# Differential attention as one pipeline over heads, placed between the query and value weights of a two-block transformer kernel

## What is computed

```python
h = rms_norm(x, g_pre_mix[1])
k, v = shared_kv(x, g_kv, w_kv)                       # rms_norm(x, g_kv) @ w_kv, split into k and v
q = (h @ w_q)                                         # 8 heads, 2 halves of 64, per head
logits = einsum(q, k) * scale + bias[dist]            # for each half m = 0, 1
logits = where(dist >= 0, logits, -inf)
probs = softmax(logits)
attn = probs[:, :, 0] - lam * probs[:, :, 1]
o = rms_norm(attn @ v, subln_g) * (1.0 - lambda_init) # per head
mix = o @ w_o
x = x + rms_norm(mix, g_post_mix[1])
```

## Time and profile before

| what | us |
|---|---|
| median of 3 runs | 1398.59 |
| lowest and highest | 1395.29 to 1399.53 |
| profiled execution | 1391.52 |
| its span | 1389.5 |
| PE busy, share of the span | 96% |
| DVE busy | 66% |
| ACT busy | 52% |

### The profile page before, as it was taken

How to read it: one execution, slowest core, us unless ns; L and a number is a source line. 1 busy time by engine, 2 the same in 40 slices (tenths; PEclk the granted TensorE clock), 3 DMA queues, 4 the chain that set the end, 5 groups by cost and what they waited for, 6 DMA issues and landing times.

```text
span 1389.5 us, 25078 instructions
## 1 busy us (share of the span) xinstructions
PE 1330.0 (96%) x10558; PEld 1288.7 (93%) x10558; DVE 918.8 (66%) x1505; ACT 725.1 (52%) x1219; POOL 4.5 (0%) x13
## 2 busy tenths in 40 slices
PE   5998899999998999999999999999999999999996
PEld 5897679999998999999999999999987799999996
DVE  4687655765446777444875999746564546999654
ACT  5754234665332666334545666646453446666644
POOL 1000000000000000000000000000000000000000
PEclk9999979999999999999999999999898999999997
DMA  6232005555552465654753666663272133666630
GB/s 257 85 122 81 31 3 150 182 180 170 181 170 75 145 200 175 194 183 129 227 180 118 194 187 196 200 200 106 89 246 66 31 109 106 201 193 192 204 121 31
DMA packets 58415, 205.20 MB, mean 148 GB/s; under 512 B 6328, under 2 KB 8640, under 8 KB 58048
## 3 DMA queue, kind: packets, MB, share of 16 engines
q1 hardware_dynamic: 56816, 201.77, 46.0%
q10 hardware_dynamic: 1488, 1.85, 0.5%
HBM read 202.53 MB, written 1.06 MB: 147 GB/s over the span
## 4 chain that ended last, share of the span: by engine, by line
PE 85%; DVE 8%; ACT 5%; issue 1%; DMA 1%; ACTq 0%; DVEq 0%
PE PS L340 65%; PE PS L385 7%; PE PS L351 2%; PE PS L368 2%; PE PS L419 2%; PE PS L2020 1%; PE PS L2019 1%; ACT WH L318 1%; DVE WL L325 1%; PE PS L466 1%; PE PS L652 1%; DMA HB<-bias_rows 1%; DVE Z L1417 1%; PE PS L784 0%; PE PS L690 0%
## 5 line engine op out<-in xcount | busy, mean ns | idle before, releaser
L325 DVE TENSOR_TENSOR WL<-RAW,WH 128x1024 fp32r<-128x1024 f32 (+2 forms) x383 | 460.5, 1207 | 261.5 <-ACT WH L318 261.2
L318 ACT ACTIVATE WH<-RAW 128x1024 fp32r<-128x1024 f32 (+2 forms) x383 | 391.2, 1042 | 251.3 <-PE PS L340 222.0
L340 PE MATMUL PS<-UH,WH 128*128 128x256 f32 (+1 forms) x1624 | 462.9, 285 | 6.9 <-DVE UL L1402 3.0
L340 PE MATMUL PS<-UH,WL 128*128 128x256 f32 (+1 forms) x1624 | 462.6, 285 | 0.0
L340 PE MATMUL PS<-UL,WH 128*128 128x256 f32 (+1 forms) x1624 | 462.4, 285 | 0.0
L340 PEld LDWEIGHTS PS<-UH,WH 128*128 128x128 f32 x1624 | 309.1, 190 | 7.9 <-issue 4.7
L340 PEld LDWEIGHTS PS<-UH,WL 128*128 128x128 f32 x1624 | 309.1, 190 | 0.0
L340 PEld LDWEIGHTS PS<-UL,WH 128*128 128x128 f32 x1624 | 307.5, 189 | 0.0
L340 PE MATMUL PS<-HL,WH 128*128 128x272 f32 (+1 forms) x512 | 145.8, 285 | 0.0
L340 PE MATMUL PS<-HH,WH 128*128 128x272 f32 (+1 forms) x512 | 145.7, 284 | 0.0
L340 PE MATMUL PS<-HH,WL 128*128 128x272 f32 (+1 forms) x512 | 145.4, 284 | 0.0
(11 more groups left out here) (346 smaller groups left out, 1976.9 us busy)
## 6 DMA issues: line engine op xcount, KB each, us to landing
RAW<-wpack SPq DMA_DIRECT2D x365, 512.0 KB, 3.6
RAW<-wpack SPq DMA_DIRECT2D x16, 384.0 KB, 3.5
X<-xin SPq DMA_DIRECT2D x1, 1088.0 KB, 5.1
C<-cst SPq DMA_DIRECT2D x1, 1072.0 KB, 10.0
HB<-bias_rows ACTq DMA_DIRECT2D x1, 1024.0 KB, 7.4
out<-X SPq DMA_DIRECT2D x4, 256.0 KB, 2.3
RAW<-wpack SPq DMA_DIRECT2D x2, 256.0 KB, 3.5
PI<-pin ACTq DMA_DIRECT2D x2, 256.0 KB, 3.1
```

Source lines behind the costliest of these rows:

```text
L318: a.e.activation(WH[n % NH][:, 0:w], RAW[n % NR][:, 0:w], ACT.Copy).then_inc(*a.mark("wh", n))
L325: v.e.tensor_tensor(WL[n % NH][:, 0:w], RAW[n % NR][:, 0:w], WH[n % NH][:, 0:w].bitcast(f32), ALU.subtract).then_inc(*v.mark("wl", n))
L340: ins = t.e.matmul(o, part(n, hw, kw, a, b), x(kx), start=first and not i and not p, stop=last and i == len(kcs) - 1 and p == 2)
```

## The change

1. **Order of weights**: for each group of 256 columns, one query unit, two value units, one query unit, in place of all value units and then all query units.
2. **Keys and queries are split.** DVE multiplies the key with the root into `TQ` (a slot of `TMA`, four in turn), ACT copies it to `KHH`, DVE subtracts to `KHL`; for queries `QHH` and `QHL` (three slots). The bias read back is split to `HBH` and `HBL`. `scores` becomes five fp32r matmuls in place of two fp32 ones, for each half and each of two row blocks.
3. **One loop over heads**, `for s in range(9)`: query(s), turn(s-2), scores(s-1), value(s), attend(s-2) on PE. The bias matmul stands before the keys and its DMAs early in the key stage. `AA` is gone: the combination overwrites `EE`.
4. **In the key stage** ACT and DVE each go unit by unit through weight split, key parts and query operand.
5. **Output by heads**: the first four output units run at once, feature block by feature block (`output`), with turn, attend and normed of the last heads between them; the other four follow as before.
6. **Embedding step**: its last pair of blocks goes through sigmoid, product and square one block at a time, its gain (`embed_gain`) moves behind the root; the first 40 fillers are gone, 12 stand between `root_begin` and `root_end`.

The diff, cut to its core:

```diff
@@ weight_units
             proj("k", "w_kv_2", None, 0, 1024)
-            rows("v", "w_kv_2", None, 1024, 2048)
-            proj("q", "w_q_2", 0, 0, 1024)
+            for g in range(4):
+                proj("q", "w_q_2", 0, 256 * g, 256 * g + 128)
+                rows("v", "w_kv_2", None, 1024 + 256 * g, 1280 + 256 * g)
+                proj("q", "w_q_2", 0, 256 * g + 128, 256 * g + 256)
@@ scalar_ffn
+                square(a, f"ple{layer}", 1, u, MM2[:, 2 * u:2 * u + 2, :], S)
+                embed_gain(a, layer, u)
+            def last_step():
...
+                for m in range(2):
+                    a.wait_ge("gz", layer, 3, m)
+                    a.e.activation(TMA[:, 2 + m, 0:S], TMA[:, 2 + m, 0:S], ACT.Sigmoid).then_inc(*a.mark("sig", layer, 3, m))
...
+                for m in range(2):
+                    a.wait_ge("pg", layer, 3, m)
+                    a.e.activation(SQ[1][:, m, 0:S], MM2[:, 6 + m, :], ACT.Square).then_inc(*a.mark("sq", ple, 3, m))
@@ tensor_diff
-            keep_going(t, 40)
-            root_sum(t, "ple0", 1, S, ("mr", "kv", 6))
+            root_begin(t, "ple0", 1, S, ("mr", "kv", 6))
             banks.hold(("root", "ple0"))
+            keep_going(t, 12)
+            root_end(t, "ple0", 1, S)
             root_spread(t, "ple0", S)
-            keep_going(t, 18, "ple0")
+            t.e.matmul(PS[0:8, b, 0:384], RBX[:, :], HOT, start=True, stop=True).then_inc(*t.mark("dif", "gr"))
+            keep_going(t, 16, "ple0")
...
-            root_spread(t, "kv", S)
             for j in range(8):
                 if j > 3:
+                    b = banks.take(t, ("k", j), ("tq", j))
                     products(t, PS[:, b, 0:S], n0 + j, pairs, 0, 128, uh, ul, u_ready).then_inc(*t.mark("dif", "k", j))
+                if j == 4:
+                    root_spread(t, "kv", S)
...
-                        t.e.matmul(o, c2("anti"), hb, start=True, stop=False)
-                        ins = t.e.matmul(o, QH[ps_, h, q0:q0 + 128], KH[ps_, h, 0:w], start=False, stop=True)
+                    for o, q0, k0, w in ((PS[:, b0 + m, 0:128], 0, 128, 128), (PS[:, b0 + m, 128:384], 128, 0, 256)):
+                        t.e.matmul(o, ANTI[:, :], HBH[:, h, k0:256], start=True, stop=False)
+                        t.e.matmul(o, ANTI[:, :], HBL[:, h, k0:256], start=False, stop=False)
+                        for p, (q_, k_) in enumerate(((QHH, KHH), (QHL, KHH), (QHH, KHL))):
+                            ins = t.e.matmul(o, q_[ps_, h % 3, q0:q0 + 128], k_[ps_, h, 0:w], start=False, stop=p == 2)
...
+            for s in range(9):
+                if s < 8:
+                    query(s)
+                if s > 1:
+                    turn(s - 2)
+                if s:
+                    scores(s - 1)
+                if s < 8:
+                    value(s)
+                if s > 1:
+                    attend(s - 2)
+
+            normed(0)
+            normed(2)
...
+            output(range(0, 4))
+            turn(7)
             normed(4)
+            output(range(4, 6))
+            attend(7)
+            keep_going(t, 16, done=("t", 7))
             normed(6)
+            keep_going(t, 12, done=("t", 7))
+            output(range(6, 8)).then_inc(*t.mark("omm", "do", 1, 0, 1))
...
+            tensor_output(t, "mix", "do", ("mr", "ffn1", 6), uh, ul, o_ready, first=2)
@@ scalar_diff
+            act_split(a, n0 + 6)
             root_sqrt(a, "kv", S)
+            act_split(a, n0 + NH)
             root_keep(a, "kv", 0, S)
             for j in range(8):
...
+                if j:
+                    act_split(a, n0 + j + NH)
+                high("k", j, KHH[:, j, :])
+                split_hi(a, ("qx", j), XH[:, j, :], X_(j), g("gpm1", j))
...
+            for s in range(9):
+                if s < 8:
+                    if s % 2 == 0:
+                        act_split(a, unit_at["q", s] + NH)
...
+                    high("q", 8 + s, QHH[:, s % 3, :])
+                if s in (0, 2):
+                    bias(2 * s)
+                if s > 1:
+                    turn(s - 2)
+                if s == 8:
+                    roots(0, 6)
+                if s:
+                    scores(s - 1)
+                if s < 8 and s % 2 == 0:
+                    act_split(a, unit_at["v", s] + NH)
+                if s < 8:
+                    value(s)
+                if s > 1:
+                    attend(s - 2)
+                if s < 8 and s % 2:
                     act_split(a, unit_at["q", s] + NH)
@@ vector_diff
+            for j in range(8):
+                if j:
+                    dve_split(v, n0 + j + NH)
+                v.wait_ge("dif", "k", j)
+                v.wait_ge("rk", "kv")
...
+                v.e.tensor_tensor(TQ(j), PS[:, banks.at["k", j], 0:S], RR[0][:, 0:S], ALU.mult).then_inc(*v.mark("tq", j))
+                if j:
+                    split_lo(v, ("qx", j - 1), XL[:, j - 1, :], X_(j - 1), g("gpm1", j - 1), XH[:, j - 1, :])
+                low(j, KHL[:, j, :], KHH[:, j, :], "khl", j)
+            split_lo(v, ("qx", 7), XL[:, 7, :], X_(7), g("gpm1", 7), XH[:, 7, :])
...
+            for s in range(9):
+                if s < 8:
+                    if s % 2 == 0:
+                        dve_split(v, unit_at["q", s] + NH)
+                    query(s)
+                if s in (0, 2):
+                    bias(2 * s)
+                if s:
+                    scores(s - 1)
+                if s < 8:
+                    low(8 + s, QHL[:, s % 3, :], QHH[:, s % 3, :], "qhl", s)
+                    if s % 2 == 0:
+                        dve_split(v, unit_at["v", s] + NH)
                 if s == 8:
+                    roots(0, 6)
+                    scaled(0)
+                if s:
+                    combine(s - 1)
+                if s > 1:
+                    attend(s - 2)
+                if s < 8 and s % 2:
+                    dve_split(v, unit_at["q", s] + NH)
```

342 lines of the change are left out of this document (174 added, 168 removed).

## The result

| | before | now |
|---|---|---|
| median, us | 1396.9 (4 runs) | 1410.7 (4 runs) |
| lowest and highest | 1394.3 to 1399.5 | 1407.7 to 1412.7 |
| profiled execution | 1391.5 | 1407.7 |
| its span | 1389.5 | 1405.9 |
| PE, DVE, ACT busy | 96%, 66%, 52% | 95%, 66%, 52% |

The ratio of the times is 1.0097, with a 95% interval of 1.0068 to 1.0125. The two profiled executions differ by 16.2 us, the medians by 13.8. Slower was the likeliest side of the forecast, and 1410.7 lies just inside the upper edge of its range (1411). But its middle, 1401.7, is 9 us short, and those 9 us need an explanation.

The account below looks back on a forecast made before the run. PE was taken to bound the kernel. Terms -22.6 + 16.2 + 1.85 + 2.8 + 3.7 + 1.85 + 0 + 0.3 - 1.0 = +3.1 us on the median before, 1398.6, gave 1401.7; range 1394 to 1411.

Parts of the forecast that it names:

- straight work, a head's scores: PE, heads: 2.24 us for a head's scores in place of 4.0; all straight work up to last scores -22.6 us.
- entry and key stage, start of value 0: First embedding step +0.3 us; key stage +16.2 us, since query(0) waits for the last XL until 1028.0.
- clock behind it: PE's clock falls behind the key stage's wait and again behind the wait at s = 2: +1.85 us each.
- wait at s = 2: Loop over heads: DVE's subtractions, query and second bias half delay the maxima, so turn(1) holds PE for +3.7 us.
- waits at s = 4, 6, 8: Loop over heads: 0.8 us of wait at s = 4 and 6, 1.2 us at s = 8; together +2.8 us.
- clock in the last scores: Last scores of the loop: no clock fall charged there, 0 us.
- tail: Last scores to last output sums: 45.6 us against 45.7, so 0, between -4 and +2.
- end: End of the kernel: gain copies and half a square leave the path to the root, -1.0 us (-0.6 to -1.5).
- ACT and DVE taking turns: Key stage: the two engines work one after the other, 3.49 us a round for seven rounds.
- one between the halves of the output products: Tail: third output group waits for banks 0 and 1 until ACT has read them, 3.4 us.
- Rival A: Scores: narrow fp32r matmuls cost a plain fp32 pass, 0.21 us; +8.0 us, 1409.7 in all; chance 0.25.
- the size of a clock fall: PE's clock: 1.85 us lost wherever PE starves for over 2 us, taken from the two queries behind an earlier gap.

Follow-up runs that it names:

- e3: Changed kernel with each head's 20 score matmuls reordered: bias ones in two groups of four, query by key ones in two groups of six; median 1398.7 us, ratio 1.0018.
- e7: Changed kernel with all eight XH and XL made before the root of the key stage, nothing else moved; median 1405.0 us, ratio 1.0055 to the kernel before.
- e2: Changed kernel with value block 0 in front of query 0 on PE; median 1413.9 us, ratio 1.0128 to the kernel before.
- e4: Changed kernel with the second half of the bias split at s = 3 and DVE's value unit subtraction behind the combination; median 1402.3 us, ratio 1.0041.
- e12: Changed pipeline with plain fp32 scores, early XH and XL, copies ahead, value unit moved, other banks, reordered tail; median 1387.7 us, ratio 0.9947 to the kernel before.

## Why the prediction came out as it did

The sum was +3.1 us, the profiled difference is +16.4. Term by term:

| term | forecast | measured | how seen |
|---|---|---|---|
| straight work, a head's scores | 2.24 us | 3.62 | 8 x 1.38 = +11.0 over the forecast |
| entry and key stage, start of value 0 | 1028.3 | 1029.3 | +1.0; a round is 3.39 us, forecast 3.49 |
| clock behind it | 1.85 | 0.6 | value 0 takes 3.57 us, the others 2.95: -1.2 |
| wait at s = 2 | 3.7 | 1.97 | -1.7 |
| clock behind it | 1.85 | 4.4 | 10.2 us at 1.2 GHz: +2.6 |
| waits at s = 4, 6, 8 | 2.8 | 2.25 | -0.6 |
| clock in the last scores | 0 | 0.8 | 4.44 us in place of 3.63: +0.8 |
| tail | 0 | -0.2 | from the last scores to the sums 45.5 us, before 45.7 |
| end | -1.0 | -1.2 | -0.2 |

The corrections add up to 11.5 us, with the 3.1 to 14.6 of the 16.4. Of the other 1.8 us, 0.8 are the second half of a change of height: the next value matmul starts 0.23 us behind the first (1039.61 to 1039.84) in place of 0.12, at seven blocks that stand behind a head's scores. Another 0.5 are five queries behind a product with V (2.83 us or more in place of 2.73), where the height stays and the width changes, and 0.4 are query 1 (3.15 us).

**Right.** That the gain of the heads' straight work is eaten in the key stage, by ACT and DVE taking turns, with the period to 0.1 us; PE's largest wait in sum for `XL` (8.9 us in four waits, though the longest single one, 2.61 us, is for `MM` in the tail); a wait before the second turn and one between the halves of the output products released by ACT (2.46 us, forecast 3.4); a tail that comes out even.

**The step that failed** is the price of a head's scores. "A head's scores are 10 fp32r matmuls of 256 columns, 0.114 us each, and 10 of 128 columns" put together prices from runs of *like* matmuls. The two prices are right: the transposes of the earlier trace rows gave the narrow one well. The 81 ns that the Trainium skill gives for the form ("TensorE: Matmul & The Clock Gate", section "Back-to-back issue gap") isn't seen here: 0.11 us. What has no term is the mix of 128 and 64 rows: each change costs 0.15 to 0.21 us, and there are 8 in a head. None of the rivals was this. Rival A came nearest in time (its mark was 3.2 us a head) and was wrong in cause: it took the narrow form to be dear. That 1410.7 still lies inside the range is luck in this sense: the range reached that far for rival A's sake. The rows of before held a hint that I passed over: a narrow plain pair with the bias, then one by query and key, 0.31 and 0.42 us, unlike prices for equal columns. The same changes of height stand in the scores of before.

**The second** is the size of a clock fall. I charged 1.85 us each time, from a stretch of queries. Those rows catch only the end of it. The window from where the clock fell, in the trace of the kernel before:

```profile
1041.10:1051.30 10.20, 10.20 (x31) 0.50 0.14 58
```

The clock was down for 10.2 us there too, first over head 0's scores (7.01 us in place of 4.08) and then over half of the two queries. By these rows the fall had cost 2.9 + 1.85, some 4.8 us, much like the 4.4 behind the turn at s = 2. The prediction had taken the slow scores out of the old time and charged only the queries' part for each new fall. Such stretches aren't all alike: behind e3's wait of 3.89 us PE was at 1.2 GHz for 6.8 us, behind e7's of 11.73 for 11.4. What sets their length isn't shown.

**What I had wrong about the key stage**, although its total fitted: that `XL` alone held PE. e2 and e7 show that the way to `QHL` of the first head held it equally.

## What to carry to other kernels

Count changes of height between neighbouring matmuls, not only matmuls: order a block so that operands of equal height stand together, and matmuls on disjoint halves of the rows as neighbours; that alone gave back 11 of 16 us here. Before filling an idle stretch or removing a wait, follow the helpers' chains to the *next* thing the busy engine will want; if that is equally late, the gain turns into a wait, and a wait of 2 us cost twice its own length again in clock (4.4 us behind 1.97). Price a fall of the clock from where it falls to where it is back, not from the part that looks cleanest. In a stage where two engines hand each operand back and forth, let one run a step ahead and serve the first consumer first.

## What the hardware showed that I hadn't expected

- A matmul of 64 rows next to one of 128 rows: 0.15 us for each change when the next has 128 columns, 0.19 to 0.21 when it has 256 (fp32r; 3.62, 3.10 us a head with 8, 4 changes). At each change the weight load starts with its matmul, not 0.06 us or more ahead.
- Two matmuls on rows 0 to 63 and 64 to 127, into different banks, start within 0.01 us of each other and overlap; twelve take 0.89 us.
- PE busy without a gap, on a turn, scores and what follows, stayed at 1.2 GHz for 10.2 us, behind a wait of 1.97 us; so it did in the kernel before behind one of 2.25. Over the same work without the wait in front (e4) the clock stayed up.
- The same instructions ahead of this stage ended up to 5.0 us apart in the traces of different kernels (first key matmul 985.25 in the changed kernel, 990.27 in e12), so a gain of a few us has to be read between two points of one trace. In the traces that came late (988.1 to 990.3) the clock had also been down near 66 us from the start (0.50 to 0.72 from 66 to 69, in all seven); in the early ones, 985.3 to 986.1, it was up there (1.00 in all six, and in the kernel before).
